# The gate tiles of the second layer as one stage of seven block products, with the next heads' values and queries as filler

## The reference

```python
h = _rmsnorm(x, pre_g)
proj = jnp.einsum('bld,de->ble', h, w_in)
z_ssm, xbc, dt_raw, q, k, v, f_raw, z_att, g_ssm, g_att = jnp.split(proj, ...)
xbc = jax.nn.silu(_causal_dwconv(xbc, conv_w, conv_b))
xs, b_ssm, c_ssm = jnp.split(xbc, ...)
dt = jax.nn.softplus(dt_raw + dt_bias)
y = _ssd_chunked(xs, dt, a, b_ssm, c_ssm, d_skip)      # 16 heads, 4 groups, chunks of 128
y_ssm = rmsnorm_by_group(y * jax.nn.silu(z_ssm)) * ssm_norm_g
log_f = jax.nn.log_sigmoid(f_raw + fgate_b)
o = _forgetting_attention(q, k, v, log_f)              # 16 heads of 64, causal, + cumsum(log_f)
y_att = o * jax.nn.silu(z_att)
merged = jax.nn.sigmoid(g_ssm) * (y_ssm @ w_branch_ssm) + jax.nn.sigmoid(g_att) * (y_att @ w_branch_att)
return x + _rmsnorm(merged @ w_out, post_g)
```

## Time and profile before

| | us |
|---|---|
| three runs | 2784.73, 2787.71, 2799.85 |
| median | 2787.71 |
| the profiled execution | 2800.11, span 2798.3, mean granted clock 0.971 |
| PE busy | 2613.4 (93%) |
| DVE, ACT, POOL busy | 1510.3, 1155.2, 1018.5 |

### The profile page before, as it was taken

How to read it: one execution, slowest core, us unless ns; L and a number is a source line. 1 busy time by engine, 2 the same in 40 slices (tenths; PEclk the granted TensorE clock), 3 DMA queues, 4 the chain that set the end, 5 groups by cost and what they waited for, 6 DMA issues and landing times. The chain is left out here.

```text
span 2798.3 us, 33571 instructions
## 1 busy us (share of the span) xinstructions
PE 2613.4 (93%) x13094; PEld 2172.8 (78%) x13094; DVE 1510.3 (54%) x2243; ACT 1155.2 (41%) x1741; POOL 1018.5 (36%) x677
## 2 busy tenths in 40 slices
PE   5999998989999999999899999999999999979995
PEld 3787877877888887787787787788888888868884
DVE  6654897376555556647634636155444554453334
ACT  3334886244444432334342423254444544441121
POOL 0212433328787744342323313223222232243222
PEclk9999999999999999999999999999999999989997
DMA  6232001213222247352212121211111011135431
GB/s 256 67 130 95 1 1 61 87 41 106 76 91 83 76 147 262 121 162 83 100 68 83 53 85 44 83 34 58 53 61 61 31 68 53 61 136 181 158 120 60
DMA packets 73229, 251.74 MB, mean 90 GB/s; under 512 B 8144, under 2 KB 8272, under 8 KB 73072
## 3 DMA queue, kind: packets, MB, share of 16 engines
q1 hardware_dynamic: 73072, 249.59, 25.4%
HBM read 203.82 MB, written 45.74 MB: 89 GB/s over the span
## 5 line engine op out<-in xcount | busy, mean ns | idle before, releaser
L2944 POOL TENSOR_TENSOR hl<-raw,hl 128x1024 fp32r<-128x1024 f32 x165 | 404.6, 2455 | 1105.1 <-ACT hl L1180 1105.0
L509 PE MATMUL ps<-ht,hl 128*128 128x512 f32 x1840 | 750.6, 408 | 20.6 <-DVE ht L2093 9.9
L510 PE MATMUL ps<-ht,hl 128*128 128x512 f32 x1840 | 725.9, 394 | 0.0
L511 PE MATMUL ps<-ht,hl 128*128 128x512 f32 x1840 | 725.6, 394 | 0.0
L509 PEld LDWEIGHTS ps<-ht,hl 128*128 128x128 f32 x1840 | 352.2, 191 | 95.4 <-DVE ht L2093 9.9
L511 PEld LDWEIGHTS ps<-ht,hl 128*128 128x128 f32 x1840 | 350.7, 191 | 76.6
L510 PEld LDWEIGHTS ps<-ht,hl 128*128 128x128 f32 x1840 | 352.1, 191 | 67.4 <-issue 1.5
L3021 POOL TENSOR_SCALAR wf<-wf,st 128x1024 f32<-128x1024 f32 (+2 forms) x192 | 168.8, 879 | 354.1 <-DVE st L2230 290.0
L1180 ACT ACTIVATE hl<-raw 128x1024 fp32r<-128x1024 f32 x167 | 175.4, 1053 | 207.3 <-PE ps L511 66.1
L722 PE MATMUL ps<-cst,wf 128*128 128x128 f32 x1088 | 160.1, 279 | 30.4 <-DVE wr L2245 16.6
L722 PEld LDWEIGHTS ps<-cst,wf 128*128 128x128 f32 x1088 | 128.0, 142 | 72.5 <-issue 47.4
(11 more groups left out here) (268 smaller groups left out, 4808.3 us busy)
## 6 DMA issues: line engine op xcount, KB each, us to landing
raw<-in_wst SPq DMA_DIRECT2D x229, 512.0 KB, 3.7
wf<-scratch_rows SPq DMA_DIRECT2D x32, 512.0 KB, 5.1
scratch_g<-wf SPq DMA_DIRECT2D x22, 512.0 KB, 2.6
wf<-scratch_g SPq DMA_DIRECT2D x44, 256.0 KB, 4.4
wf<-in_xT SPq DMA_DIRECT2D x16, 512.0 KB, 8.1
htf<-in_wst SPq DMA_DIRECT2D x16, 512.0 KB, 15.5
wf<-in_wst SPq DMA_DIRECT2D x10, 512.0 KB, 4.6
scratch_x<-wf SPq DMA_DIRECT2D x8, 512.0 KB, 5.3
```

The source lines that it names most:

```text
L509: self.op.matmul(out, wh, xh[:, c], start=(j == 0), stop=False)
L510: self.op.matmul(out, wh, xl[:, c], start=False, stop=False)
L511: t = self.op.matmul(out, wl, xh[:, c], start=False, stop=(j == kt - 1))
L2944: self.op.tensor_tensor(K.hl[:, u * 2048 + 1024:u * 2048 + 2048], K.raw[:, i % 3 * 1024:(i % 3 + 1) * 1024], hi.bitcast(F32), ALU.subtract ...
```

## The change

The class of the seven products is generalised (`Seven`) and used twice, for the 20 pairs of w_up as before and for 9 pairs of tiles of the second layer. A new stage `gates` stands between `down` and `ssm`:

- The tail of `down` runs dtf, gs 0, gs 1 instead of dtf, xs 0, xs 1. `gates` then has gs 2, the turning of the rates, gs 3 and "ends", all plain, and nine pairs by seven products: gs 4 to 7, za 0 to 5, ga 0 to 5, and za 6 with ga 6. za 7 and ga 7 stay fillers of the last head pair. Raw weights have the three slots and no fourth place. DVE makes eight sums of input blocks and their eight low parts, ACT the eight high parts. The results (gs, za with its factor, ga) go to DRAM; "za" is a new buffer there.
- `ssm`: the fillers of a group are z, z and the next group's xs 2g+2 (k 0 behind the last group), 48 steps, with no flush. The norm of group g stands in the tiles xs 2g+3 and B g+1, that of the last group in v 0 and q 0.
- `attend2`: fillers are v p+1 and q p+1, both through bank 7 by halves, copied out by ACT; k p+1 stays late. Four more steps stand ahead of a pair's first scores (8, not 4), and `fills` gives the steps between the softmax steps. The queries of the next pair are stacked at step 15. The multiplication by silu of za moves to `last`, with a load of za from DRAM.
- The normed hidden state is written in place, so the first half of the residual is stored by tile f < 8 instead of 6 to 13.

The diff, cut to its core:

```diff
     s.append(("w", "dtf", 0))
+    s += [("w", "gs", n) for n in range(4)]
     for g in range(4):
         s += [("w", "xs", 2 * g), ("w", "xs", 2 * g + 1), ("w", "B", g), ("w", "C", g)]
-        s += [("w", "z", 2 * g), ("w", "z", 2 * g + 1), ("w", "gs", 2 * g), ("w", "gs", 2 * g + 1)]
-    s.append(("w", "k", 0))
-    for p in range(8):
-        s += [("w", "v", p), ("w", "q", p), ("w", "za", p), ("w", "ga", p)]
-        if p < 7:
-            s.append(("w", "k", p + 1))
+        s += [("w", "z", 2 * g), ("w", "z", 2 * g + 1)]
+    s += [("w", "k", 0), ("w", "v", 0), ("w", "q", 0)]
+    for p in range(1, 8):
+        s += [("w", "v", p), ("w", "q", p), ("w", "k", p)]
+    s += [("w", "za", 7), ("w", "ga", 7)]
...
+UP_PAIRS = [(("up", NFF + f), ("up", f)) for f in range(PLAIN, NFF)]
+GATE_PAIRS = [(("gs", 4), ("gs", 5)), (("gs", 6), ("gs", 7)), (("za", 0), ("za", 1)),
+              (("za", 2), ("za", 3)), (("za", 4), ("za", 5)), (("ga", 0), ("ga", 1)),
+              (("ga", 2), ("ga", 3)), (("ga", 4), ("ga", 5)), (("za", 6), ("ga", 6))]
...
+        self.gate = Seven(self, "gate", "ssm", ("gs", 3), GATE_PAIRS, (16, 17), 19, (18, 20),
+                          (8, 10, 12, 14))
...
+    def raw_after(self, i, t):
+
+        if self.fourth is None:
+            r = 2 * i + t
+            return ("wlo", self.last - 2 + r) if r < 3 else self.part_of((r - 3) // 2, (r - 3) % 2)
+        if i >= 2:
+            return self.part_of(i - 2, t)
+        return ("wlo", self.last - 2 + 2 * i + t) if i == 0 or t == 0 else ("lo", self.x, 7, 1)
...
+def fills(p, s):
+
+
+    if p == 7:
+        return 3
+    return 2 if s < 1 or s in (2, 4, 6, 10, 12) else int(s < 14)
...
+    def gates(self):
+
+        K = self.K
+        x = self.hidden("ssm")
+        self.run(self.dense(("gs", 2), 0, x))
+        self.empties(0, ("gtanh", 2))
+        self.to_tokens(19, [("scan", 8)], 2, "rates")
+        self.empties(2, ("tm",))
+        self.fetch(("gs", 3), 0)
+        self.run(self.dense(("gs", 3), 1, x))
+        self.empties(1, ("gtanh", 3))
+        self.consts()
+        self.wait_ge(*K.at("tm"))
+        self.bank_free(4)
+        self.op.matmul(K.ps[2][:, 0:128], K.c_last, K.tm[:, :, 32:48], start=True,
+                       stop=True).then_inc(*self.done("ends"))
+        self.emptied[4] = (("dec",), ("end",))
+        for i in range(K.gate.n):
+            self.seven(K.gate, i)
+        for b in range(4):
+            self.emptied[b] = (("gated_by", K.gate.n - 1, int(b < 2)),)
 
...
+            self.run(late)
+            for n, _ in enumerate(self.dense(("xs", 2 * g + 1), 1, x)):
+                if n in (0, 9):
+                    next(side, None)
+            self.empties(1, ("xconv", 2 * g + 1))
+            for n, _ in enumerate(self.dense(("B", g), 0, x)):
+                if n in (4, 6):
+                    next(side, None)
+            self.empties(0, ("xconv", 8 + g))
             for pr in (0, 1):
                 self.to_tokens(pr, [("xsilu", 2 * g + pr)], 2 + pr, ("x", g, pr))
...
+            late = first(g + 1)
+            self.fillers = [zs(2 * g, 0), zs(2 * g + 1, 1), late]
...
+        def raw_rows(name, p, label):
+
+            for h in (0, 1):
+                yield from self.dense((name, p), 3, x, halves=(h,), bank=1)
+                self.emptied[7] = ((label, p, h),)
...
+        late = self.late
+        self.run(late)
+        for n, _ in enumerate(self.dense(("v", 0), 3, x)):
+            if n in (0, 9):
+                next(self.side)
+        self.empties(3, ("vraw", 0, 0), ("vraw", 0, 1))
+        for n, _ in enumerate(self.dense(("q", 0), 0, x)):
+            if n in (4, 6):
+                next(self.side)
+        self.empties(0, ("qraw", 0, 0), ("qraw", 0, 1))
...
+            if p < 7:
+                self.fillers = [raw_rows("v", p + 1, "vraw"), raw_rows("q", p + 1, "qraw")]
+                late = after_fillers(self, self.keys(p + 1))
+            else:
+                self.fillers = [silu_z(p), gate(p)]
+                late = None
+            self.fill(8)
...
+        rates()
+        self.fetch(("gs", 2), 1)
+        tanh(0)
+        tanh(1)
+        self.sum_high(st, 2)
+        self.sum_high(st, 3, ("stored_r1",))
+        self.sum_high(st, 1)
+        self.sum_high(st, 4)
+        self.fetch(("gs", 3), 0)
+        self.wait_ge(*K.at("turned", "rates", 1))
+        self.op.activation(w(23), K.ps[2][:, :], ACT.Copy).then_inc(*self.done("tm"))
+        self.weights_high(st, 0, 0, 1)
+        tanh(2)
+        self.weights_high(st, 0, 2, 3)
+        tanh(3)
+        self.wait_ge(*K.at("ends"))
+        self.op.activation(K.dec[:, :], K.ps[2][:, 0:128], ACT.Exp).then_inc(*self.done("dec"))
+        self.wait_ge(*K.at("end"))
+        self.op.activation(K.end[:, :], K.end[:, :], ACT.Exp).then_inc(*self.done("endexp"))
+        self.weights_high(st, 0, 4, 5, 6)
...
+        def raw_half(name, p, h, i, bank, label):
+            self.wait_ge(*K.at("full", name, p, h))
+            self.op.activation(w(i)[:, HALF[h]], bank,
+                               ACT.Copy).then_inc(*self.done(label, p, h))
+
+        def values(p):
+            self.fetch(("v", p))
+            for h in (0, 1):
+                yield from steps(7)
+                self.wait_ge(*K.at("turned", ("v2", p - 1), 1))
+                raw_half("v", p, h, 8, K.bank(7), "vraw")
+                yield
+
...
+                if s == 15 and p < 7:
+                    self.wait_ge(*K.at("scores", 2, g))
+                    self.wait_ge(*K.at("qraw", p + 1, 1))
+                    self.stack_high(w(23), (0, 1), ("q2", p + 1), 0.125)
...
+            for t, i, j, ready in ((1, 3, 1, ()), (3, 0, 3, (1,)), (2, 0, 1, (3, 1)), (4, 4, 2, (2,))):
+                for m in (0, 1):
+                    for n in range(8):
+                        self.wait_ge(*K.at("lo", "ssm", n, 1))
+                    for r in ready:
+                        self.wait_ge(*K.at("t", "gate", r, 2 * m))
+                    x = (st.value(i, m) if i else
+                         v3(w(4 + 2 * m, 2), 1024)[:, :, HALF[1]])
+                    self.op.tensor_tensor(st.value(t, m), x, st.value(j, m),
+                                          ALU.subtract).then_inc(*self.done("t", "gate", t, 2 * m))
+                    self.mark("t", "gate", t, 2 * m + 1)
...
-            self.wait_ge(*K.at("out", 2, 8 * p + 7))
-            self.wait_ge(*K.at("zasilu", p, 1))
-            self.op.scalar_tensor_tensor(out=w(22), in0=w(22), scalar=0.5, in1=w(23), op0=ALU.mult,
-                                         op1=ALU.mult).then_inc(*self.done("ya", p))
...
+            x = w(2 * n + 1)
+            self.wait_ge(*K.at("ya_in", n))
+            self.wait_ge(*K.at("za_in", n))
+            self.op.scalar_tensor_tensor(out=x, in0=x, scalar=0.5, in1=w(16 + n % 4), op0=ALU.mult,
+                                         op1=ALU.mult).then_inc(*self.done("ya", n))
+            self.low(x, K.wrr(2 * n), K.wrr(2 * n + 1), 0, "ya", n, 0)
...
```

1080 lines of the change are left out of this document (560 added, 520 removed).

## The result

| | before | after |
|---|---|---|
| runs compared first, median (range) | 2793.78 (2784.73 to 2801.99, 4 runs) | 2765.39 (2762.23 to 2767.61, 4 runs) |
| the same two kernels compared again | 2787.5 (2782.82 to 2800.72, 23 runs) | 2770.51 (2763.59 to 2773.27, 6 runs) |
| span of the profiled execution | 2798.3 | 2765.8 |

What follows compares the result with a forecast made beforehand. PE's issue plus its holes was taken as the bound. Terms -24.5 (matmuls), -2, +3.3, -8.0, +4.6 and +1.4 sum to -25.2 us, from a median of 2787.71 to 2763 us, range 2746 to 2781.

Steps and rivals of the forecast that it cites:

- no gain: Nine pairs in the new stage: POOL and the third raw slot pace them, chain 21.7 us, time 2787; chance 0.05.
- The head of the stage: Start of the new stage: holes of 5.7 us before gs 2 and 2.8 before the first product; together -2 us.
- Scan groups: Scan stage: PE waits 1.1 us for the late norm multiplication in three groups, +3.3 us, bounds 0 to +9.
- From scan to attention: Change from scan to attention: waits of 3.1 and 1.4 us and lost clock go, -8.0 us, bounds -10 and 0.
- Head pairs: Seven attention pairs: the stacked queries' wait of 9.5 us goes, bank stops and less filler come; +4.6 us, bounds -9 and +25.
- The seams: Halves of v and q sharing one bank: PE stops for ACT's copy, 1.5 us per pair, 10.5 in seven.
- the thin filler: Head pairs from s = 1 on: four to five fewer steps between softmax steps, 0.5 us per pair, 3.5 in all.
- The last pair: Last head pair: four steps stand before the scores, not behind, so its tail grows; +1.4 us, bounds 0 and +5.
- The price of two SBUF inputs: Rival: sixteen new DVE operations at the stage's head take 2.27 us, not 1.23; +5 us, 2768; chance 0.08.
- the cheap case: Stage's head: the new DVE operations take 1.23 us each, argued from POOL being busy only 22 of 68 us.
- The larger gain: Rival in the head pairs: the shared bank's stops and fewer filler steps cost nothing, -12 us, 2751; chance 0.14.
- the slower case: Rival: a head pair becomes bound by its softmax chain, 56 us of holes in seven pairs, 2819; chance 0.05.

Runs made afterwards that it cites:

- the eighth product: The last product of each gate pair computed twice, 12 matmuls more per pair, against the changed kernel: 2790.04 us, ratio to before 1.0002.
- the tanh experiment: ACT's tanh of gs 0 moved right behind the bias of the rates, ahead of their abs, exp and log, against the changed kernel: 2768.42 us.

## Why the prediction was right, and which terms were not

The forecast is right for its main reason: 24.5 us are the matmuls (the eighth product), PE is full in the nine pairs, and POOL and the third slot have room. The rival "no gain" is out by its own mechanism. The rest of the sum was forecast at -0.7 us and came as -5.8 in the traces, by errors that partly cancel.

- The head of the stage: both holes right to 0.3 us, the first with its releaser, the second by luck. Its releaser is DVE's subtraction behind the tanh and the sigmoid of gs 3, and the table load that the prediction counted in it is not there. The view behind the first hole was not complete: I priced the hole as ACT's order, and the tanh experiment shows that DVE's chain stands behind it with nearly the same price.
- Scan groups: the wait of 1.1 us came as 1.06, at the place that was named. The holes grew by 3.3 us, the forecast. The term is +1.0, since the clock loss in the groups is 3.4 us smaller in the second trace, which the edit did not cause as far as the runs show.
- From scan to attention: -5.9 and not -8.0. The two waits of the earlier trace rows went, 4.5 us, and the clock loss fell by 5.1, where 3.4 were forecast; but k 0 as filler takes the bank pair of z 7, and PE waits 2.43 us for its gating at 1885, a wait that the old order, with gs 6 in another pair of banks, did not have. The step that failed is "k 0 is filler now" at no cost.
- Head pairs: -4.9 and not +4.6. The seams were sized well: 0.41 and 0.69 us, 1.1 per pair against 1.5. The mis-sized term is the thin filler, put at +0.5 us per pair: instead the second and third wait of an old pair, 1.2 and 0.8 us, went. I had left both standing. They did not go by the eight steps (with four, the second did not return). The trace before puts the second down to the silu of za in DVE's list (L2809), which left the pairs with its tile; for the third the cause is open. The parts that I had priced make +4.5 by their own numbers, not +4.6, and pair 0 alone took 2.9 us more than each of the others, which I had not foreseen.
- The last pair: +5.0 and not +1.4. The holes grew by 3.7 us, and the clock loss of the piece stayed as it was. Its filler has the seam exactly at the eight steps, 2.51 us, with a clock of 0.66 from 2400 to 2405; four steps get back 1.3 to 3.1 us of it. The rest is the price of too little filler.
- The price of two SBUF inputs was real (3.35 for 1.22 us) and cost PE nothing at the head. The argument for the cheap case was read from the wrong trace: POOL was busy for 22 of 68 us there before and for 51.5 now. The sixteen operations took 1.42 and 1.70 us each, which is 5.3 of the 16.6 us extra, and it was room in the chain that saved PE, since with the tanh moved it did cost some 2 us. In the pair, where one such operation was put back, the price was 1.5 us (2.72 for 1.23) of a damage of 8. The rival's own sum is a little off as well: scans that end 8.3 us after 1320.8 are 2.1 us late for 1327, not 1.8.
- The larger gain, all seams and the thin filler at no cost, is -14 by the terms 10.5 and 3.5, not -12: 2748.5.

The worst step is one that the result doesn't show. I called the slower case unlikely, since DVE's 43 and ACT's 41 us of an old pair "would still fit into 67". Busy time was the wrong view: the pair's floor, in this order of the fills, is 63.5 us with both engines at 61 to 63%. Of the 21.7 us that left a pair all came through, but some nine matmuls more, 2 us, and the rest would have bought nothing. A chance of 5% for that rival was too low.

## What to carry to other kernels

Where filler is taken out of a latency-bound loop, the engines' busy shares do not tell how much may go; cut the filler by a third and by two thirds in a trial and read the floor. When an operation is moved, look at the stores that wait for it and at the loads that stand behind those stores in the issuing queue. When one bank is shared by half tiles, let the halves change between two fills.

## What the runs showed of the hardware

- A DVE operation with two SBUF inputs took 1.22 us alone, 1.96 to 3.35 us beside POOL's work (16x1024), and 1.23 against 2.72 us (128x1024). One with a single tile and a column as inputs took 0.74 and 1.43 us.
- A hole of 2.8 us on PE is in some executions followed by 5 us at a clock of 0.50 to 0.72 and in others not, with the same instructions around it. Over three scan groups this was worth 5 us.
